# Gate and branch products turned round: token tiles stand still, weights stream, and y is turned back by TensorE

## The reference

```
xn = _rmsnorm(x, norm_pre_w[l])
h = xn @ w_in[l]
na_q, na_k, na_v, na_z, hg_q, hg_ff, hg_fb, hg_i, hg_z, gate_pre = jnp.split(h, splits, axis=-1)
...                      # o_a: neighbourhood attention, o_b: two gated scans
g = jax.nn.sigmoid(gate_pre + b_gate[l])
g_a, g_b = jnp.split(g, N_BRANCHES, axis=-1)
y = g_a * (o_a @ w_branch[l, :NA_WIDTH]) + g_b * (o_b @ w_branch[l, NA_WIDTH:])
x = x + _rmsnorm(y @ w_out[l], norm_post_w[l])
```

## Time and profile before

| | |
|---|---|
| median of 3 runs | 802.03 us |
| the profiled execution | 801.79 us |
| its span, first to last instruction | 800.0 us |
| TensorE matmul busy | 792.0 us (99%) |
| VectorE busy | 621.0 us (78%) |
| ScalarE busy | 391.8 us (49%) |
| DMA queue of the weights | 151.05 MB, 65.1% of the 16 engines' span |

### The profile page before, as it was taken

One profiled execution on the slowest core, in us unless ns is written; L12 is line 12 of the kernel. 1 busy time (PEld: TensorE's weight loads), 2 busy tenths in 40 slices (PEclk: granted clock), 3 DMA queues, 4 the chain that ended last, 5 costly groups with the idle time before them and its releaser, 6 DMA issues.

```text
span 800.0 us, 13827 instructions
## 1 busy us (share of the span) xinstructions
PE 792.0 (99%) x5636; PEld 688.5 (86%) x5636; DVE 621.0 (78%) x1103; ACT 391.8 (49%) x666; POOL 25.7 (3%) x45
## 2 busy tenths in 40 slices
PE   9999999999999999999999999999999999999996
PEld 7888888888888888888888888888888888888885
DVE  6687558889889889889889889889875887864543
ACT  7665454445445445445445445445445555554442
POOL 5000000000000000000000000000000000000002
PEclk9999999999999999999999999999999999999999
DMA  9976397757657657657667657667667776577522
GB/s 326 395 234 213 109 259 200 191 160 199 187 160 201 182 162 204 179 163 204 178 165 205 176 165 206 174 167 198 166 167 197 219 205 180 189 244 281 176 89 107
DMA packets 239280, 155.62 MB, mean 195 GB/s; under 512 B 3952, under 2 KB 220272, under 8 KB 238576
## 3 DMA queue, kind: packets, MB, share of 16 engines
q1 hardware_dynamic: 238352, 151.05, 65.1%
q10 hardware_dynamic: 864, 3.68, 1.2%
HBM read 151.56 MB, written 2.10 MB: 192 GB/s over the span
## 4 chain that ended last, share of the span: by engine, by line
PE 99%; DVE 0%; POOL 0%; ACT 0%; DVEq 0%; issue 0%; POOLq 0%
PE psum L1161 48%; PE psum L1169 25%; PE psum L1213 10%; PE psum L1398 4%; PE psum L1397 4%; PE psum L1396 4%; PE psum L1183 2%; PE psum L1309 1%; PE psum L1279 1%; PE psum L1257 1%; PE psum L1298 1%; PE psum L1244 0%; PE psum L1175 0%; PE psum L1271 0%; PE psum L1318 0%; DVE big L1122 0%
## 5 line engine op out<-in xcount | busy, mean ns | idle before, releaser
L722 DVE TENSOR_TENSOR w_lo<-raw,w_hi 128x1024 fp32r<-128x1024 f32 x268 | 317.4, 1221 | 65.1 <-ACT w_hi L484 65.0
L1161 PE MATMUL psum<-act_hl,w_hi 128*128 128x512 f32 x1408 | 335.9, 391 | 0.0
L1161 PEld LDWEIGHTS psum<-act_hl,w_hi 128*128 128x128 f32 x1408 | 258.8, 188 | 50.1
L484 ACT ACTIVATE w_hi<-raw 128x1024 fp32r<-128x1024 f32 x268 | 270.5, 1053 | 58.4 <-PE psum L1398 27.0
L1169 PE MATMUL psum<-act_hl,w_lo 128*128 128x256 f32 x1408 | 184.8, 284 | 0.0
L1169 PEld LDWEIGHTS psum<-act_hl,w_lo 128*128 128x128 f32 x1408 | 178.7, 191 | 5.0
L498 ACT ACTIVATE part<-psum 128x256 f32<-128x256 f32 x88 | 33.8, 384 | 232.0 <-PE psum L1169 232.0
L1161 PE MATMUL psum<-branch_hl,w_hi 128*128 128x512 f32 x256 | 61.1, 391 | 0.0
L1213 PE MATMUL psum<-w_hi,branch_hl 128*128 128x512 f32 x224 | 55.4, 390 | 0.0
L1161 PEld LDWEIGHTS psum<-branch_hl,w_hi 128*128 128x128 f32 x256 | 47.0, 188 | 9.1
L1396 PE MATMUL psum<-w_hi,act_hl 128*128 128x512 f32 x128 | 49.8, 389 | 0.0
(11 more groups left out here) (132 smaller groups left out, 569.1 us busy)
## 6 DMA issues: line engine op xcount, KB each, us to landing
raw<-in_w_in SPq DMA_DIRECT2D x100, 1024.0 KB, 5.8
raw<-in_w_branch SPq DMA_DIRECT2D x16, 1024.0 KB, 5.9
raw<-in_w_out SPq DMA_DIRECT2D x16, 1024.0 KB, 5.1
raw<-in_w_in SPq DMA_DIRECT2D x8, 256.0 KB, 6.2
raw<-in_w_in SPq DMA_DIRECT2D x4, 512.0 KB, 9.1
big<-in_x_rows SPq DMA_DIRECT2D x2, 1024.0 KB, 14.9
big<-in_x_rows ACTq DMA_DIRECT2D x2, 1024.0 KB, 6.2
big<-in_x_turned SPq DMA_DIRECT2D x7, 256.0 KB, 7.3
```

The source lines that it names most:

```text
L484: nc.scalar.activation(w_hi[:, (2 * r + h) % HALVES, :], raw[:, r, 1024 * h:1024 * (h + 1)], ACT.Copy).then_inc(hi_ready, 1)
L722: nc.vector.tensor_tensor(w_lo[:, i, :], raw[:, r, 1024 * h:1024 * (h + 1)], w_hi[:, i, :].bitcast(F32), ALU.subtract).then_inc(lo_ready, 1)
L1161: nc.tensor.matmul(sums[h][:, :], w_hi[:, i, w], operand[:, k, :], start=k == 0 if whole else k % 8 == 0, stop=False, skip_group_check=True)
```

## The change

Gate tiles (24 in the groups, 8 in the tail) and branch tiles (16) are multiplied token-major by a new function `token_tile`, 512 rows by 512 columns a tile, four tiles to a block. Sums lie with tokens on partitions, two PSUM banks a block; high and low parts add up in the sum, so `take_part` and the first addition go for these tiles. The gate bias is now a value per column: ScalarE's queue loads it, the same for all partitions, into the place where the gates will lie, and VectorE adds the sum to it. In the branch stage the merge works on token rows, and y, now token-major, is turned by 32 transposes on TensorE (`turn_y`); its high and low part are made from the turned sums in PSUM. The slots of a group are set in another order (the first gate tile third, z eighth). The small products get other PSUM banks; the scores now come behind the value product and the near recurrence scores.

```diff
+NSLOT_Q, NSLOT_K, NSLOT_G0, NSLOT_F, NSLOT_B, NSLOT_HQ, NSLOT_G1, NSLOT_Z, NSLOT_G2, NSLOT_HZ = range(10)
+GATE_HOMES = ((16, 18), (20, 22), (24, 26), (0, 2), (4, 6), (8, 10), (28, 12), (14, 30))
+BIAS_TIMES = {(0, 8): 0, (1, 8): 1, (2, 8): 2, (3, 8): 3, (5, 0): 4, (7, 0): 5, (7, 8): 6}
...
-        ps_scores = psum[:, 0:2, 0:2 * BAND]
-        ps_o, ps_tr = bank[2:4]
-        ps_proj, ps_lvl = bank[4:6], bank[6:8]
+        ps_scores = psum[:, 4:6, 0:2 * BAND]
+        ps_o, high_slot = (psum[:, 4 + i, 2 * BAND:2 * BAND + T] for i in range(2))
+        ps_tr = bank[7]
+        ps_proj = bank[0:2]
+        def gate_sums(b):
+            return bank[0:2] if b == GATE_BLOCKS - 1 else bank[2:4]
...
+            def load_gates(g, s):
+                load(r, w_in_v[:, 4 * part_k:4 * part_k + 4, col:col + 512], n)
...
-                    load(r, w_branch_v[:, :, bass.ds(jj * (RAW * P) + r * P, P)], jj * RAW + (N_IN + r))
+                    load(r, w_branch_v[:, 4 * r:4 * r + 4, 512 * c:512 * (c + 1)], N_IN + c * RAW + r)
...                                                          ScalarE
+            def gate_bias(b):
+                for t in range(2):
+                    act.dma_start(gate(b, t), b_gate[b].partition_broadcast(P)).then_inc(bias_home[b], 16)
+            def gate_tanh(b):
+                for t in range(2):
+                    act.wait_ge(gate_out, 2 * b + t + 1)
+                    nc.scalar.activation(gate(b, t), gate(b, t), ACT.Tanh, scale=0.5).then_inc(gate_ready, 1)
...
-                take_part(place(NG, t)[0], t % 2)
+                if t == 6:
+                    act.wait_ge(hg_out, NG)
+                    gate_bias(GATE_BLOCKS - 1)
             hgrn_hi(NG - 1)
+            gate_tanh(GATE_BLOCKS - 1)
+            def split_y(c):
+                for u in range(2):
+                    act.wait_ge(y_turned, 2 * c + u + 1)
...                                                          VectorE
+            def take_gates(g, s):
+                b, part_k = gate_tile_of(g, s)
+                if part_k == 3:
+                    dve.wait_ge(half_used, 2 * place(g, s)[0] + 2)
+                    dve.wait_ge(bias_home[b], 2 * 16)
+                    for t in range(2):
+                        nc.vector.tensor_tensor(gate(b, t), gate_sums(b)[t], gate(b, t), ALU.add).then_inc(gate_out, 1)
+            def gated(out, b, sums):
+                for t in range(2):
+                    dve.wait_ge(gate_ready, 2 * b + t + 1)
+                    nc.vector.scalar_tensor_tensor(out=out[t], in0=gate(b, t), scalar=1.0, in1=sums[t],
                                                    op0=ALU.add, op1=ALU.mult).then_inc(y_step, 1)
+            def merge_first(c):
+                dve.wait_ge(half_used, 2 * (N_IN + c * RAW + 2))
+                gated(y_tok[c % 2], c, branch_sums(c, 0))
+            def merge_second(c):
+                dve.wait_ge(half_used, 2 * (N_IN + c * RAW + 4))
+                wait(dve, y_sum, 2 * c)
+                gated(y_other, c + 4, branch_sums(c, 1))
+                for t in range(2):
+                    dve.wait_ge(y_step, 4 * c + t + 3)
+                    nc.vector.tensor_tensor(y_tok[c % 2][t], y_tok[c % 2][t], y_other[t], ALU.add).then_inc(y_sum, 1)
...
                     split_next(c * RAW + (N_IN + N_BR + r), r)
+                    if (c, r) == (0, 0):
+                        merge_second(3)
+                    if (c, r) == (0, 1):
+                        split_y(3)
...                                                          TensorE
+            def token_tile(n, operand, sums, part_k, begin, end, between):
+                def product(t, h, kk, lo, weights, start=False, stop=False):
+                    k, w = 4 * part_k + 2 * h + kk, slice(kk * 512, (kk + 1) * 512)
+                    return nc.tensor.matmul(sums[t][:, :], operand[:, k, lo * T + t * P:lo * T + (t + 1) * P],
+                                            weights[:, (2 * n + h) % HALVES, w], start=start, stop=stop)
+                for h in range(2):
+                    pe.wait_ge(hi_ready, n * 2 + h + 1)
+                    for t in range(2):
+                        for kk in range(2):
+                            product(t, h, kk, 0, w_hi, start=(begin and h == 0 and kk == 0))
+                            product(t, h, kk, 1, w_hi)
+                between()
+                for h in range(2):
+                    pe.wait_ge(lo_ready, n * 2 + h + 1)
+                    for t in range(2):
+                        for kk in range(2):
+                            ins = product(t, h, kk, 0, w_lo, stop=(end and h == 1 and kk == 1))
+                    ins.then_inc(half_used, 1)
...
+            def turn_y(c):
+                pe.wait_ge(y_sum, 2 * c + 2)
+                for u in range(2):
+                    for kk in range(2):
+                        for t in range(2):
+                            w = slice((2 * u + kk) * P, (2 * u + kk + 1) * P)
+                            ins = nc.tensor.matmul(branch_sums(c, 0)[u][:, kk * T + t * P:kk * T + (t + 1) * P],
+                                                   y_tok[c % 2][t][:, w], block[:, 0, :], start=True, stop=True,
+                                                   is_transpose=True)
+                    ins.then_inc(y_turned, 1)
```

More of the change, by code:

```diff
@@ L1382, in _ @@
[L1382 to L1385 removed]
+                gate_tile(NG, t, lambda: visits(NG, t))
+            def turn_y(c):
+                pe.wait_ge(y_sum, 2 * c + 2)
+                for u in range(2):
+                    for kk in range(2):
[5 more added lines that the diff above has]
+                    ins.then_inc(y_turned, 1)
@@ L1386, in _ @@
+            for c in range(4):
                 for r in range(RAW):
-                    branch(jj * RAW + (N_IN + r), r, jj * RAW + r)
+                    branch_tile(c, r)
             def out_sums(c, t, r, h):
```

308 lines of the change are left out of this document (155 added, 153 removed).

## The result

The changed kernel takes 812.77 us (median of 4 runs, 812.40 to 813.33); the kernel before took 801.93 us on the same chip (801.50 to 802.18). The ratio is 1.0138, with a 95% interval of 1.0125 to 1.0151. The profiled execution has a span of 811.5 us against 800.0. The forecast was 798.9 us and faster; it was wrong in sign, and by 14 us.

The account below looks back on a forecast made before the run. TensorE, busy 792.0 of 800.0 us, was taken to bound the kernel by the sum of its matmuls. Tiles -6.1, transposes +2.8 and wait +0.2 gave -3.1 us: 802.03 became 798.9 us, range 797.7 to 801.0.

Parts of the forecast that it names:

- the rivals: Four alternatives: turns of y wait (0.12), transposes cost full duration (0.04), token tiles cost channel price (0.03), last bias late (0.02).
- The saving of a bare tile: Gate and branch tiles: token-major 5.440 us against channel-major 5.567, 0.127 us gained a tile, 6.1 us for 48.
- The formula of the Trainium skill: TensorE matmul takes N / 2.4 ns plus 2.5 ns; by it a turned tile would gain only 0.02 us.
- The transposes: Turning y on TensorE, 32 transposes in four turns of eight: 0.70 us a turn, 2.8 us added, between 2.6 and 3.7.
- The visits: Small products in each group: same ones, scores only later; -0.8 to +0.8 us from shape change-overs, taken as 0.
- The hand-over to `w_out`: Fourth turn of y, end of first `w_out` tile: TensorE and its inputs arrive together; 0.2 us wait, between 0 and 1.5.
- The biases: Sixteen 256 KB loads on ScalarE's queue, costed at nothing; a load twice the size had landed in 8.8 us.
- The second rival: Turning y: each transpose costs its whole 0.271 us, 8.7 us for 32; 804.8 us, slower; chance 0.04.
- the third's channel cost: Rival on gate and branch tiles: among channel tiles a token tile costs their 5.567 us, nothing saved; 805.0 us; chance 0.03.
- the forecast's own range: Whole kernel: 797.8 to 799.9 us if the forecast itself holds, chance 0.79.
- its signs for "wrong": Longer TensorE wait at first `w_out` or second branch tile, turned tiles over 5.5 us, transposes 0.1 us apart, branch clock below 1.

Follow-up runs that it names:

- mended padded kernel: Changed kernel plus always-satisfied TensorE waits ahead of halves in groups and early tail, more in group 0 than the first padding: 799.73 us, ratio 0.9976 to the kernel before.

## Why the prediction was wrong

**The step that failed** is the first: "So no engine, queue or buffer holds TensorE up, and the time is the sum of its matmuls. Only two things can move it: what TensorE issues, and new waits in a stream that has had none." The reading of the profile was right for the kernel before, but it was made a rule for the kernel after. There was a third thing, the supply of the instructions. It left no wait in the kernel before because its eight visits fell into the good places. That was luck, and it was close: moved by 28 instructions the same kernel loses time, and moved by 112 it is 25 us slower, 3.3 of them by the longer warm-up. The page did show the queue, with 45 transfers of 16 KB, and it was passed over. "In a group the small products are the same ones" was true, and costing them at nothing missed that it is not only what is issued that counts, but how many instructions stand ahead of it. None of the rivals had it, and it is worth 13.3 of the 14 us by which the forecast missed.

**The other terms** can be held against the mended padded kernel, which has the whole change and of the pauses only the 0.5 us in the tail. Its stages begin at these places in the timeline of PE:

```profile
93.33 1.98 PE L1232 MATMUL psum<-act_hl,w_hi 128*128 128x512 f32 x8
...
613.69 2.66 PE L1248 MATMUL psum<-w_hi,branch_hl 128*128 128x512 f32 x11
...
644.52 1.03 PE L1474 MATMUL psum<-block,hg 128*128 128x128 f32 x8
645.31 2.07 PE L1248 MATMUL psum<-w_lo,branch_hl 128*128 128x512 f32 x8
...
703.43 0.39 PE L1510 MATMUL psum<-w_hi,act_hl 128*128 128x512 f32 x1
```

| stage | before | mended padding | difference | forecast |
|---|---|---|---|---|
| groups and tail | 523.34 | 520.36 | -3.0 | -4.1 |
| branch stage | 89.07 | 89.74 | +0.7 | 16 x -0.127 + 3 x 0.70 = +0.1 |
| `w_out` to the last start | 86.84 | 87.72 | +0.9 | +0.7 + 0.2 |
| span | 800.0 | 798.5 | -1.5 | -3.1 |

- The saving of a bare tile was right: 5.44 us in a run of its like; among channel tiles 5.47, with 5.54 instead of 5.57 for the channel tile behind it, which is the same sum. The formula of the Trainium skill that the prediction set against its rows ("TensorE: Matmul & The Clock Gate", section "Back-to-back issue gap") is given there for a single matmul by itself; for a stream of 512-column ones the section has about 131 ns, and no stretch here shows that either (227 to 229 ns). The sum did not rest on it.
- The transposes were mis-sized: 3.5 us instead of 2.8. The 0.07 us was misread. The 0.14 us that I halved run from the first transpose to the next product, and the trace of the kernel before has the two transposes at 261.751 and 261.859 us, 0.108 apart, the same as the eight in a row here. With it the tile's 0.23 us more would have given 7 x 0.108 + 0.12 = 0.88 us a turn, and 0.89 was measured. I chose the lower end of my own bounds, and the right value stood near the upper, 0.92 a turn. A turn of 0.89 us times four eats more than the sixteen branch tiles save (2.0 us): the branch part of this change is a loss of 1.5 us by itself, and all the gain is in the gates.
- The visits were costed at nothing, "so -0.8 to +0.8 us, and I take 0". The groups and the tail gained 1.1 us less than the tiles should give. 0.5 us of it is the pause in the tail. The other 0.6 us is 0.07 in each group, 59.52 us instead of 59.83 - 0.38 = 59.45, and 0.1 in the tail. It does not lie in the visit: the gate tile ahead of it and the tile that holds it take 5.47 + 8.57 us for 5.57 + 8.60, the full 0.13 less. It lies in the two gate tiles that hold small products themselves, with the tile behind each: 6.40 + 5.55 us for 6.47 + 5.57, and 5.72 + 5.54 for 5.80 + 5.57. Why these save less was not taken apart, and stays open.
- The hand-over to `w_out` was given 0.2 us and needed none.
- The biases landed in 4.4 us, and no rival came true. The second rival's 0.271 us a transpose was 2.5 times too much, the third's channel cost did not appear.
- Together: -6.1 + 3.5 + 0.6 + 0 = -2.0 us; with the 0.5 us of the tail's pause -1.5, the difference of the spans, and with the 13.3 us lost in the changed kernel +11.3, where its span is 11.5 longer.
- The upper end of the forecast's own range was added up wrongly: turns at 3.7 us with 0.5 of wait give 802.03 - 6.1 + 3.7 + 0.5 = 800.1 us, and not 799.9.

Without the pauses the forecast's range (797.7 to 801.0) would have held the 799.73 us, and its direction too. With them, of its signs for "wrong" only one showed, starts 0.1 us apart, and that one explains 0.7 us; it had been there in the trace of the kernel before. The real sign, waits whose releaser is "issue", was not on the list.

## What to carry to other kernels

When an engine is at 99% and waits for nothing, ask also how its instructions reach it: count them in pieces of the size that the instruction queue's line gives, and find the stretches in which some 320 pass in under 7 us. Every stretch of 321 ahead of a pause had passed in 1.9 to 6.8 us up to the stop, and no stretch that passed without one was shorter than 6.0 us. If there are such stretches, any edit that changes the number of instructions ahead of them, be it a tile in another form or the warm-up, can cost or win some per cent, and a comparison of two kernels is read only after the waits marked "issue" have been looked at. The cures that worked here are to break the stretch up with large products, where that costs little, or to pad the loop to a whole number of pieces with waits that are already satisfied.

## What the runs showed of the hardware

- TensorE's instructions arrive 256 at a time, 16 KB. Of the 31 gaps seen in or just behind the visits of eight kernels (0.39 to 3.99 us from start to start), every one ended at an instruction whose number leaves 193 modulo 256, 1.12 to 1.64 us after the end of a transfer. That the places from about 42 to 172 hurt, and those from 179 over 255 to 24 do not, holds for this visit of some 360 instructions; from 32 to 35 one kernel paused (0.48 us at 32) and others passed (34, 35). In the tail's visit of some 290 the places 126, 156 and 166 hurt, and 44, 72 and 108 did not.
- With the gaps of 3.99 and 3.35 us in the changed kernel, in which TensorE did nothing, came a granted clock of 0.5 (1.2 GHz) for 6.8 and 3.4 us (of the 6.8 us, 1.6 lie inside the pause); that cost 4.3 us on top of 6.8 us of waits. Behind its gaps of 1.41 and 0.95 us the clock stayed at 1. It is no fixed price: in the kernel without bias loads the same gap of 3.99 us was followed by 3.4 us at half clock, and of the two gaps of 3.10 us in the kernel moved by 112 one was followed by 3.4 us and the other by none, though its gaps of 2.04 and 2.54 us were.
- A satisfied wait that stands as an instruction of its own took 51 ns in the trace and cost nothing beside products of 0.227 or 0.119 us: 276 of them left a group at 59.52 us. Not all written waits become instructions, 276 of 348 did.
- Eight fp32 transposes of 128 x 128 in a row start 0.109 us apart and cost 0.108 us each, with 0.27 us as the duration of one.
